# Three orders of work in a one-core transformer kernel: the next product ahead in projections, high parts ahead of squares in output products, splits and heads ahead of the last pair's sums

## The reference, cut to what matters

```
x = x + 0.5 * g * swiglu(modulate(rms(x), shift, scale), wi, wo)      # pre, layers 0 and 1; ctx too
q, k, v = split(modulate(rms(x)) @ w_qkv); q = rope(rms_gain(q)); k = rope(rms_gain(k))
x = x + g2 * (attention(q, k, v) @ w_o)                                # a: differential, b: windowed
x = x + 0.5 * g3 * swiglu(...)                                         # post
...
proj = rms_norm(x, g_mix) @ w_in; x = x + norms(attention(...)) @ w_out; x = x + peer_ffn(rms_norm(x, g_ffn))
```

## Time and profile before

| | |
|---|---|
| median of 3 runs | 2922.61 us (2922.25 to 2923.37) |
| profiled execution | 2922.47 us, of which its span is 2920.6 us |
| TensorE matmul busy | 2796.7 us, 96% of the span |
| VectorE busy | 1663.5 us, 57% |
| ScalarE busy | 1203.8 us, 41% |
| GpSimd busy | 181.2 us, 6% |
| granted TensorE clock, mean | 0.983 of full |
| moved from and to memory | 152 GB/s over the span |

### The profile page before, as it was taken

How to read it: one execution, slowest core, us unless ns; L and a number is a source line. 1 busy time by engine, 2 the same in 40 slices (tenths; PEclk the granted TensorE clock), 3 DMA queues, 4 the chain that set the end, 5 groups by cost and what they waited for, 6 DMA issues and landing times.

```text
span 2920.6 us, 46554 instructions
## 1 busy us (share of the span) xinstructions
PE 2796.7 (96%) x16356; PEld 2356.1 (81%) x16356; DVE 1663.5 (57%) x2852; ACT 1203.8 (41%) x1953; POOL 181.2 (6%) x142
## 2 busy tenths in 40 slices
PE   7999999998999999999998899997899999999999
PEld 4777887755878888888886689995899999888888
DVE  3333348756633335333357665686598777677765
ACT  4322224345422323223234554455444555455544
POOL 2000003200100001000021010000061000000000
PEclk9999999999999999999999999998999999999999
DMA  7544331254343232332333545640466555677764
GB/s 269 185 173 167 107 101 65 81 188 164 116 152 99 92 108 93 99 97 92 107 100 133 208 157 179 221 163 22 156 211 204 171 171 175 207 240 240 242 201 140
DMA packets 144836, 445.18 MB, mean 152 GB/s; under 512 B 16080, under 2 KB 44880, under 8 KB 144208
## 3 DMA queue, kind: packets, MB, share of 16 engines
q1 hardware_dynamic: 112896, 409.51, 42.7%
q10 hardware_dynamic: 31824, 34.09, 3.3%
HBM read 428.33 MB, written 15.20 MB: 152 GB/s over the span
## 4 chain that ended last, share of the span: by engine, by line
PE 85%; DVE 7%; ACT 3%; issue 2%; DMA 2%; SPq 1%; POOL 0%; ACTq 0%; DVEq 0%
PE bank L1932 22%; PE bank L1933 21%; PE bank L1934 21%; PE bank L2432 12%; PE bank L2404 2%; PE bank L1949 2%; DVE w_lo L1193 2%; ACT w_hi L662 1%; PE bank L2300 1%; PE bank L2205 1%; DVE stage_rs L1394 1%; SPq L564 1%; PE bank L2139 1%; PE bank L2152 1%; DMA raw<-w_stream_dram 1%
## 5 line engine op out<-in xcount | busy, mean ns | idle before, releaser
L1932 PE MATMUL bank<-H,w_hi 128*128 128x256 f32 (+1 forms) x3344 | 1110.4, 332 | 22.7 <-DVE H L1229 11.6
L1193 DVE TENSOR_TENSOR w_lo<-raw,w_hi 128x1024 fp32r<-128x1024 f32 x605 | 739.8, 1225 | 653.0 <-ACT w_hi L662 645.9
L1934 PE MATMUL bank<-H,w_lo 128*128 128x256 f32 (+1 forms) x3344 | 1083.3, 324 | 0.0
L1933 PE MATMUL bank<-H,w_hi 128*128 128x256 f32 (+1 forms) x3344 | 1083.1, 324 | 0.0
L662 ACT ACTIVATE w_hi<-raw 128x1024 fp32r<-128x1024 f32 x628 | 660.3, 1052 | 217.3 <-PE bank L1934 175.3
L1932 PEld LDWEIGHTS bank<-H,w_hi 128*128 128x128 f32 x3344 | 642.1, 192 | 103.9 <-issue 42.0
L1933 PEld LDWEIGHTS bank<-H,w_hi 128*128 128x128 f32 x3344 | 642.3, 192 | 53.0 <-issue 4.9
L1934 PEld LDWEIGHTS bank<-H,w_lo 128*128 128x128 f32 x3344 | 641.4, 192 | 49.6
L1932 PE MATMUL bank<-act_hi,w_hi 128*128 128x512 f32 (+1 forms) x770 | 267.4, 347 | 0.0
L1934 PE MATMUL bank<-act_hi,w_lo 128*128 128x512 f32 (+1 forms) x770 | 266.9, 347 | 0.0
L1933 PE MATMUL bank<-act_lo,w_hi 128*128 128x512 f32 (+1 forms) x770 | 266.9, 347 | 0.0
(11 more groups left out here) (232 smaller groups left out, 2539.8 us busy)
## 6 DMA issues: line engine op xcount, KB each, us to landing
raw<-w_stream_dram SPq DMA_DIRECT2D x704, 512.0 KB, 3.4
ada_side<-w_stream_dram SPq DMA_DIRECT2D x52, 512.0 KB, 4.2
gelu_scratch<-gelu ACTq DMA_DIRECT2D x108, 128.0 KB, 3.6
gelu_in<-gelu_scratch ACTq DMA_DIRECT2D x108, 128.0 KB, 3.5
ada_start<-w_stream_dram SPq DMA_DIRECT2D x16, 512.0 KB, 13.9
bias<-bias_in_dram ACTq DMA_DIRECT2D x1, 3072.0 KB, 10.8
X<-x_in_dram SPq DMA_DIRECT2D x1, 2048.0 KB, 10.4
mem<-mem_in_dram SPq DMA_DIRECT2D x1, 1024.0 KB, 16.9
```

Source lines behind the costliest of these rows:

```text
L1193: nc.vector.tensor_tensor(w_lo[:, s, :], raw[:, s, :], w_hi[:, s, :].bitcast(F32), ALU.subtract).then_inc(lo_ready, 1)
L1932: nc.tensor.matmul(to, w_hi[:, s, cut], hi, start=first, stop=False, skip_group_check=True)
L1933: nc.tensor.matmul(to, w_hi[:, s, cut], lo, start=False, stop=False, skip_group_check=True)
L1934: return nc.tensor.matmul(to, w_lo[:, s, cut], hi, start=False, stop=last, skip_group_check=True)
```

## The change

It writes four pieces of the order anew; products, tiles and their number stay.

1. **Start.** ACT squares all eight chunks of X into a buffer of their own (`x_squares`, in the space of H), DVE adds them up, and TensorE sums over features with one matmul in place of eight. TensorE takes chunk 0 of the first three `wi0` tiles after modulation group 2 and chunk 1 after group 3, ahead of the second turn. The modulated whole is made by DVE (`shifted`), not by POOL, and the norm's DVE part is written out. SP issues the fourth `wi0` tile and `mem` only when the last modulation group has landed.
2. **Projections.** TensorE's step k is now: product k+1, sum of tile k-1, rotation of tile k-2. ACT's and DVE's orders stay.
3. **End of attention a.** ACT makes all three splits ahead of the last pair's `o_out`, and the heads 0 to 2 ahead of the late root; DVE makes `scaled(3)`, `low(0)`, `scaled(4)` and `low(1)` ahead of the last pair's sums.
4. **Output products of x alone.** ACT's row m is: split of tile m+3, then squares of row m-1.

```diff
             def attend_a():
...
                     if u < last:
                         exps(u)
+                    if u == last:
+                        split(splits[0])
+                        root_table()
+                        root(0, EARLY_HEADS)
+                    if u == last + 1:
+                        split(splits[1])
+                        split(splits[2])
                     p = values_due(u, 0)
                     if p is not None:
                         o_out(p)
-                    if u >= last:
-                        split(splits[u - last])
-                    if u == last:
-                        root_table()
-                        root(0, EARLY_HEADS)
-                high(0)
+                for c in range(3):
+                    high(c)
                 root(1, LATE_HEADS)
-                for c in range(1, KC):
+                for c in range(3, KC):
                     high(c)
...
             def project_out(stage, halves, update):
+                if halves == "LC":
+                    for m in range(KC):
+                        rows_out(update, m, next_splits(stage, update, m))
+                    return
                 for m in range(KC):
-                    rows_out(update, m, next_splits(stage, update, m))
+                    for t in next_splits(stage, update, m)[0]:
+                        split(t)
+                    if m:
+                        squares(update, m - 1, "L")
+                squares(update, KC - 1, "L")
...
                 split(splits[2])
-                o_squares(KC - 1)
-                variance(LATE_HEADS)
                 scaled(3)
                 low(0)
                 scaled(4)
+                low(1)
+                o_squares(KC - 1)
+                variance(LATE_HEADS)
+                scaled(5)
+                low(2)
                 turn_root(1, LATE_HEADS)
...
+                def shifted(c):
+                    for half in range(HALVES):
+                        ins = nc.vector.tensor_scalar(stage_y[:, c % 2, half * NT:(half + 1) * NT],
+                                                      z_buf(c)[:, half * NT:(half + 1) * NT], n["scale"](c, half),
+                                                      n["shift"](c, half), ALU.mult, ALU.add)
+                    ins.then_inc(y_ready, 1)
...
+                for c in range(1, KC):
+                    dve.wait_ge(x_squared, c + 1)
+                    if c > 1:
+                        dve.wait_ge(x_added, c - 1)
+                    nc.vector.tensor_tensor(x_squares[:, 0, :], x_squares[:, 0, :], x_squares[:, c, :], ALU.add
+                                            ).then_inc(x_added, 1)
...
-                for k in range(len(tiles) + 2):
-                    if k < len(tiles) and not (name and k < AHEAD):
-                        if k >= 3:
-                            pe.wait_ge(of(stage, "evac_ready"), k - 2)
...
-                        product(proj_bank(k), t0 + k, tiles[k]["halves"])
+                def tile_product(k):
+
+                    if k >= 3:
+                        pe.wait_ge(of(stage, "evac_ready"), k - 2)
...
+                    product(proj_bank(k), t0 + k, tiles[k]["halves"])
+
+                if not name:
+                    tile_product(0)
+                for k in range(len(tiles) + 2):
+                    if (AHEAD if name else 1) <= k + 1 < len(tiles):
+                        tile_product(k + 1)
                     if 1 <= k <= len(tiles) and tiles[k - 1]["kind"] == "n":
...
-            for n in range(len(ADA_ORDER)):
-                start_product(n)
-                if n % 2 == 1:
-                    start_turn(n // 2)
+            pe.wait_ge(x_added, KC - 1)
+            nc.tensor.matmul(bank[0][:, :], ones, x_squares[:, 0, :], start=True, stop=True).then_inc(x_summed, 1)
+            start_product(0)
+            start_product(1)
+            start_turn(0)
+            start_product(2)
+            first_chunks(range(0, 1))
+            start_product(3)
+            first_chunks(range(1, 2))
+            start_turn(1)
```

More of the change, by code:

```diff
@@ L1528, in attend_a @@
                 scaled(4)
+                low(1)
[3 more added lines that the diff above has]
+                low(2)
                 turn_root(1, LATE_HEADS)
-                for c in range(1, KC):
+                for c in range(3, KC):
+                    if c + 3 < KC:
+                        scaled(c + 3)
                     low(c)
-                    if c + 4 < KC:
-                        scaled(c + 4)
             def attend(pair):
@@ L1626, in adjust, with first_norm, z, low @@
                 return ins
-            def first_half():
-                start_store(0)
-                dve.wait_ge(mod_stored, 1)
-                adjust(0, (1,), (), range(0, 4)).then_inc(mod_ready, 1)
-                for n in range(AHEAD):
-                    split(RING["wi0"] + n)
-            def second_half():
-                start_store(1)
-                dve.wait_ge(mod_stored, 2)
-                adjust(0, (1,), (), range(4, KC)).then_inc(mod_ready, 1)
-            norm("pre0", {1: first_half, 3: second_half})
+            def first_norm():
+                n = NORMS["pre0"]
+                rs = stage_rs[:, 0, :]
+                def z(c):
+                    if c >= 4:
+                        dve.wait_ge(hl_ready, c - 3)
+                    nc.vector.tensor_tensor(cols(z_buf(c), "LC"), X[:, :, c, :], cols(rs, "LC"), ALU.mult).then_inc(z_ready, 1)
+                def shifted(c):
[4 more added lines that the diff above has]
+                    ins.then_inc(y_ready, 1)
+                def low(c):
+                    dve.wait_ge(y_ready, c + 1)
+                    dve.wait_ge(hh_ready, c + 1)
+                    nc.vector.tensor_tensor(h_ap(1, c, "LC"), cols(stage_y[:, c % 2, :], "LC"), h_ap(0, c, "LC").bitcast(F32),
+                                            ALU.subtract).then_inc(hl_ready, 1)
+                def modulation_of(b):
+                    start_store(b)
+                    dve.wait_ge(mod_stored, b + 1)
+                    dve.wait_ge(mod_ready, b)
+                    adjust(0, (1,), (), range(4 * b, 4 * b + 4)).then_inc(mod_ready, 1)
+                    dve.wait_ge(mod_ready, b + 1)
+                for c in range(1, KC):
[4 more added lines that the diff above has]
+                                            ).then_inc(x_added, 1)
+                dve.wait_ge(rs_ready, 1)
+                link(nc.vector.reciprocal(rs, rs))
+                for c in range(4):
+                    z(c)
+                modulation_of(0)
+                shifted(0)
+                split(RING["wi0"])
+                low(0)
+                split(RING["wi0"] + 1)
+                split(RING["wi0"] + 2)
+                for c in range(1, 4):
+                    shifted(c)
+                    z(c + 3)
+                    low(c)
+                modulation_of(1)
+                for c in range(4, KC):
+                    if c + 3 == KC - 1:
+                        z(c + 3)
+                    shifted(c)
+                    low(c)
@@ L1906, in low_parts @@
                                             ALU.subtract).then_inc(lo_ready, 1)
-            for name in ("pre0", "mix_a", "qkv_a", "post0", "pre1", "mix_b", "qkv_b", "post1"):
+            for name in ("mix_a", "qkv_a", "post0", "pre1", "mix_b", "qkv_b", "post1"):
                 if name == "qkv_a":
@@ L2052, in first_products, with first_chunks @@
                             ins.then_inc(tile_used, 1)
+            def first_chunks(chunks):
+                t0 = RING["wi0"]
+                for k in chunks:
+                    pe.wait_ge(hl_ready, k + 1)
+                    for n in range(AHEAD):
+                        if k == 0:
+                            pe.wait_ge(lo_ready, split_at(t0 + n) + 1)
+                        ins = passes(bank[n][:, :], (t0 + n) % R, k, h_ap(0, k, "LC"), h_ap(1, k, "LC"), k == 0, k == KC - 1)
+                        if k == KC - 1:
+                            ins.then_inc(tile_used, 1)
             def ffn(f, name, halves, update):
@@ L2058, in steps @@
                     if isinstance(i, int) and i == 0:
-                        first_products(name, bank[0:AHEAD], t0, halves)
+                        if f:
+                            first_products(name, bank[0:AHEAD], t0, halves)
+                        else:
+                            first_chunks(range(2, KC))
                         if f == 0:
@@ L2344, in _ @@
             pe.wait_ge(cs_ready, 2)
-            for c in range(KC):
-                pe.wait_ge(sq_ready, c + 1)
-                nc.tensor.matmul(bank[0][:, :], ones, stage_sq[:, c % 2, :], start=c == 0, stop=c == KC - 1
-                                 ).then_inc(sq_used, 1)
-            for n in range(len(ADA_ORDER)):
-                start_product(n)
-                if n % 2 == 1:
-                    start_turn(n // 2)
```

(2 more changed lines are left out.)

29 lines of the change are left out of this document (16 added, 13 removed).

## The result

The changed kernel takes 2891.99 us median (2889.61 to 2892.88, 4 runs), the kernel before 2922.43 (2921.45 to 2923.37, 4 runs) beside it: ratio 0.990, 95% interval 0.9888 to 0.9911, so 26 to 33 us faster. The forecast was 2891.0. The profiled execution took 2892.88 with a span of 2891.1.

The account below looks back on a forecast made before the run. TensorE was taken to bound nearly everything, with its idle time at seven joints and the low clock behind it to win. The terms sum to 31.6 us off the profiled 2922.47, forecast 2891, range 2883 to 2900.

Parts of the forecast that it names:

- The start, 2.1 us: Kernel start: chunks 0 and 1 taken between modulation groups and turn bring chunk 2 to 42.0 us; 2.1 us won.
- qkv_a, 6.8 us: qkv_a's beginning: a product covers waits of 0.79 and 3.63 us, giving 4.4; with the clock staying up, 6.8.
- End of attention a, 4.7 us: Attention a's end: earlier splits and scaling bring out_a's first pass 2.95 us forward; higher clock behind it gives 1.7.
- qkv_b, 2.4 us: qkv_b: last product ends 5.4 us earlier, but three rounds of 3.0 us follow instead of two; 2.4 us won.
- out_b, 3.9 us, and out_c, 7.5 us: Output products: splits ahead of squares break an ACT-DVE loop; out_b 3.3 plus 0.6 for clock, out_c 8.0 less 0.5.
- proj_c, 4.2 us: proj_c: product 2 fills 2.9 us of the first squares' wait, clock returns 2.5; the tail limits the gain to 4.2.
- (a): Rival: the clock does not come back at qkv_a, attention a's end and proj_c; 6.6 us less, 2897.5; chance 0.11.
- sign of being wrong: Prediction wrong if low clock shows at those joints, or DVE's reciprocals of qkv_a stand over 7.3 us apart.
- (b): Rival: DVE takes the projections; qkv_b gives nothing, proj_c 1.5, qkv_a 4.4; 7.5 us less, 2898.5; chance 0.09.
- (c): Rival: head start holds to the end of qkv_b and proj_c, groups land earlier; 6 us more, 2885; chance 0.08.
- (d): Rival: slower, as the loop of a projected tile closes over TensorE; 2933 at 1 us per tile; chance 0.02.
- The rule weighed: Sustained TensorE activity releases the throttled clock; low in qkv_b's and proj_c's tails, sum 31.6, or 28.2 if each lost 1.7.

Follow-up runs that it names:

- run 8: The kernel before with four matmuls on constants, result unused, in TensorE's wait ahead of qkv_a's first rotation: 2919.54 us against 2922.25.
- run 3: The kernel before with the new end of attention a alone: 2915.48 us against 2921.34.
- run 10: The changed kernel with the old order in peer_q and matmuls on constants cut to fit in nine remaining waits: 2881.65 us against 2922.25 of the kernel before.
- run 7: The kernel before with seven matmuls on constants, result unused, ahead of qkv_a's first rotation: 2923.76 us against 2922.49.
- run 12: The kernel of run 10 with one more matmul on constants in each of the last waits of the three attentions: 2879.47 us against 2921.87 of the kernel before.
- run 1: The kernel before with the new start alone: 2919.63 us against 2921.34.

## Why the prediction was right, step by step

**The start, 2.1 us.** Right to where it was worked out: first pass at 34.58 (forecast 34.6), chunk 2 at 42.00 (42.0; before it stood at 44.20, forecast from its rows 44.1). Behind that the profile after gives back 0.9 us by `wo0`, mostly at TensorE's third `ada_side` group, which was issued 2.05 us earlier and came only 1.32 earlier. After, before, and run 8 with the old start:

```profile
72.46 1.06 PE L2015 MATMUL bank<-ada_side,cs 128*32 128x512 f32 x8 [1.14 <-DMA ada_side<-w_stream_dram]
...
73.78 1.06 PE L1949 MATMUL bank<-ada_side,cs 128*32 128x512 f32 x8 [0.40 <-DMA ada_side<-w_stream_dram]
...
74.58 1.06 PE L1954 MATMUL bank<-ada_side,cs 128*32 128x512 f32 x8 [1.48 <-DMA ada_side<-w_stream_dram]
```

The longer wait is not the new start's doing. It is 0.09 to 1.48 us in the six profiles with the old start and 0.14 to 1.14 in those with the new one: this group lands when it lands, and the forecast, made from one profile, had no term for that.

**qkv_a, 6.8 us.** 7.1 in every run that has the new order. Its clock term is confirmed alone (2.3, run 8); the rest is 4.8, not 4.4.

**End of attention a, 4.7 us.** 3.0 from the turn to the first pass (forecast 2.95) and 1.55 by `wo1` (1.7), in the profiles after and in run 3. The 0.7 to 1.6 us more come before that end, and no piece of the change aims at them. Nearly all of it is TensorE's waits within attention a for modulation tiles to land, 2.52 us in the profile before, 1.18 in the one after and 1.79 in its second. The first two such waits of the profile before:

```profile
612.84 1.07 PE L1949 MATMUL bank<-raw,cs 128*32 128x512 f32 x8 [0.86 <-DMA raw<-w_stream_dram]
...
620.33 1.06 PE L1949 MATMUL bank<-raw,cs 128*32 128x512 f32 x8 [1.23 <-DMA raw<-w_stream_dram]
```

In the fourteen profiles these waits sum to 0.66 to 3.12 us, with the old order and the new: the forecast is right in both its terms, and the surplus is no more than this scatter.

**qkv_b, 2.4 us.** 1.9, and 1.8 to 2.0 in every run that has the new order. The tail did change as forecast, from two rounds to three, but the rounds are 3.4 and 3.0 us, not 3.0 each. The low clock behind these waits, 10.2 us long in place of 6.8, costs next to nothing: with the tail at 1.00 in run 10 the stage gives 2.0.

**out_b, 3.9 us, and out_c, 7.5 us.** The loop was the cause: the sums follow the passes by 0.39 us of waiting. From its first pass to the first of `wo3`, out_b took 163.8 us before and 159.8 and 159.7 in the two profiles of the changed kernel, 4.0 and 4.1 us less; what the table has beside that fell on attention b's last values. out_b's sums came 3.2 and 3.4 us earlier counted from its first pass. out_c's came 7.1 us earlier with low clock inside the stage and 8.5 without, beside a forecast of 8.0 less 0.5 for the clock: the size of that last term depends on where a low stretch falls.

**proj_c, 4.2 us.** 4.0 in each of the five profiles that have the new order and no fillers, against the profile from which it was forecast, but 2.8 against the three others in which proj_c's first low stretch is the shorter one. The wait for the first squares fell by 2.87 us as forecast (2.9); the clock term of 2.5 us was read from an execution where it was large.

**Not in the sum.** peer_q, 2.1 us slower. I had listed peer_q with the change's second piece and then left it out as a stage without the chain; I priced what the move wins there, nothing, and not what it costs at the end, though I had done just that for qkv_b and proj_c. And low clock that moves: 1.4 us lost on attention b's last values in one profile, 0.9 won behind "routed". These, with the landings, cancelled within a few us, which is luck of sizes: the forecast median was hit to 1 us, its terms to between 0.2 and 1.4 us each.

**The rivals.** (a) fell: the clock came back at all three joints. The forecast's sign of being wrong did not show either: DVE's reciprocals of qkv_a stand 7.21 us apart from the third on. (b) fell for proj_c and qkv_a, and was partly so in qkv_b, where DVE has waits of only 0.35, 0.45 and 0.36 us before its last reciprocals. (c) and (d) did not come. **The rule weighed** (the Trainium skill, TensorE: Matmul & The Clock Gate, Part 1) says that activity releases the throttled state. Runs 7, 8 and 12 agree, by filling waits with matmuls whose result nobody uses: 0.51 became 1.00 behind 3.63 us of wait, and the low clock behind waits of 1.1 to 1.6 us at attention a's end became 1.00 too. By the rule, the clock was also to be low in the tails of qkv_b and proj_c, and it is, from 1554.2 and from 1946.7 us: in qkv_b at hardly a price, as run 10 shows, while no run tells proj_c's price apart.

## What to carry to other kernels

When a product can be issued ahead of the small operations that wait for a chain on other engines, count what it covers at the stage's beginning and then what is left uncovered at its end, also in stages that have no chain. At an idle stretch of TensorE look behind it, not only at it: here half as much again was lost at the low clock behind qkv_a's wait (2.3 us beside 4.8). If a wait can't be removed, a few matmuls on constants that fit in it (0.86 us each here) give that second part back (2.3 us in run 8), and nothing where another engine sets the pace; sized too long they cost what they overrun.

## What the runs showed of the hardware

Where the clock is low shifts from one execution of the same kernel to the next: 79 and 73 us at half clock in two profiles of the changed kernel, and 1.4 us lost in attention b in one of them, 0.6 won in the other; 155.9 or 154.7 us for the old proj_c. The Trainium skill (TensorE: Matmul & The Clock Gate, Part 1) says that the cold stretch at a kernel's start varies from run to run; here the same is seen in the middle of the kernel. That a stage repeats to 0.1 us in a few profiles (qkv_a, qkv_b and proj_c in the new order) does not yet make one profile of before a sure mark for it.

Group 2 of the start was taken at 29.39 to 31.62 us among the kernels with the new start (29.48 to 31.62 among those in which SP issues in the same order): transfers of a kernel's first 30 us scatter by 2 us between executions.

A late tile can cost more than its wait. At attention a's third modulation group TensorE waited 1.63 to 1.89 us in three of the fourteen profiles, and in these three, and no other, the granted clock fell at that place (0.51 from 609 to 616 us in run 1); in the eleven with waits of 0.52 to 1.50 us it stayed up.
